# A gated-delta and attention layer on one core: x handed over feature-major, and row sums in four column groups of TensorE

## The reference

```
mod = silu(c) @ ada_w + ada_b                 # c: [1, 1024], ada_w: [1024, 3072]
shift, scale, gate = split(mod, 3)
h = rmsnorm(x, pre_norm_w) * (1 + scale) + shift
proj = h @ w_in                               # 1024 x 4104: q, k, v, gate of 8 attention heads;
                                              # q, k, v, z of 4 delta heads; beta, decay
o_moba = causal attention (rope on q and k) * silu(mg)
o_dn   = rmsnorm(gated delta rule(short_conv(dq, dk, dv))) * silu(dz)
y = concat(o_moba, o_dn) @ w_out
x = x + gate * rmsnorm(y, post_norm_w)
```

## Time and profile before

| | |
|---|---|
| median of 3 runs | 201.45 us (200.59 to 201.94) |
| the profiled execution's own time | 201.38 us |
| its span in the trace | 199.2 us |
| TensorE busy | 185.7 us, 93% |
| VectorE busy | 138.4 us, 69% |
| ScalarE busy | 104.1 us, 52% |
| GpSimd busy | 83.4 us, 42% |
| read from HBM | 37.08 MB |

### The profile page before, as it was taken

The page is one execution under the profiler, slowest core; times in us unless marked ns, Lnnn a source line. Parts: engine busy times, 40 slices in busy tenths (PEclk is TensorE's granted clock), DMA queues, the critical chain, the costliest instruction groups (busy, mean ns, idle before and its releaser), DMA issues.

```text
span 199.2 us, 4716 instructions
## 1 busy us (share of the span) xinstructions
PE 185.7 (93%) x1898; PEld 170.3 (86%) x1898; DVE 138.4 (69%) x326; ACT 104.1 (52%) x201; POOL 83.4 (42%) x46
## 2 busy tenths in 40 slices
PE   7999779999999989999999999997999999899970
PEld 6897769999999989988989999896999987588850
DVE  0638989463079988979878646746989399837364
ACT  2835445636398869396553226385234548337230
POOL 2037709795969616928065003974000220504000
PEclk9988999999999999999999999999999999999998
DMA  5999999999106530197308400062029357910022
GB/s 211 394 403 404 409 396 407 400 406 408 42 0 207 175 147 0 44 396 305 105 3 273 151 3 3 3 212 106 3 74 412 151 205 223 359 59 0 3 107 105
DMA packets 11527, 38.43 MB, mean 193 GB/s; under 512 B 1393, under 2 KB 1521, under 8 KB 10994
## 3 DMA queue, kind: packets, MB, share of 16 engines
q1 hardware_dynamic: 11362, 37.61, 50.6%
q10 hardware_dynamic: 144, 0.52, 0.7%
HBM read 37.08 MB, written 1.05 MB: 191 GB/s over the span
## 4 chain that ended last, share of the span: by engine, by line
PE 51%; DVE 28%; DMA 8%; ACT 6%; issue 3%; POOL 1%; DVEq 0%; SPq 0%; ACTq 0%; POOLq 0%
PE bank L1337 11%; PE bank L1338 10%; PE bank L1339 10%; DVE cv L951 7%; DVE accg L1139 5%; DMA raw<-in_w_out 4%; PE bank L1348 4%; DVE bank L926 3%; DMA outb<-in_post_norm_w 3%; PE bank L1547 3%; PE bank L1558 3%; PE bank L1535 2%; DVE pr L1114 2%; ACT whi L544 1%; DVE ssq L1003 1%
## 5 line engine op out<-in xcount | busy, mean ns | idle before, releaser
L471 POOL TENSOR_TENSOR wlo<-raw,whi 128x1024 fp32r<-128x1024 f32 (+1 forms) x25 | 57.4, 2317 | 66.7 <-ACT whi L544 66.7
L1337 PE MATMUL bank<-hhi,whi 128*128 128x256 f32 x224 | 65.3, 292 | 3.0 <-DVE hlo L895 2.1
L1338 PE MATMUL bank<-hhi,wlo 128*128 128x256 f32 x224 | 63.6, 284 | 0.0
L1339 PE MATMUL bank<-hlo,whi 128*128 128x256 f32 x224 | 63.5, 283 | 0.0
L1337 PEld LDWEIGHTS bank<-hhi,whi 128*128 128x128 f32 x224 | 43.1, 193 | 5.2 <-DVE hlo L895 2.9
L1338 PEld LDWEIGHTS bank<-hhi,wlo 128*128 128x128 f32 x224 | 43.2, 193 | 0.0
L1339 PEld LDWEIGHTS bank<-hlo,whi 128*128 128x128 f32 x224 | 43.1, 193 | 0.0
L544 ACT ACTIVATE whi<-raw 128x1024 fp32r<-128x1024 f32 (+1 forms) x33 | 33.0, 1026 | 10.6 <-PE bank L1339 7.5
L951 DVE SCALAR_TENSOR_TENSOR cv<-bank,convh,cv 128x255 f32<-128x255 f32 (+2 forms) x36 | 17.0, 481 | 8.6 <-ACT cv L608 7.6
L926 DVE SCALAR_TENSOR_TENSOR bank<-ada,sml,bank 128x512 f32<-128x512 f32 (+1 forms) x24 | 16.5, 687 | 0.7
L485 POOL TENSOR_TENSOR rot<-rot,cst 128x512 f32<-128x512 f32 x4 | 4.4, 1091 | 22.3 <-DVE rot L1081 20.4
(11 more groups left out here) (203 smaller groups left out, 359.0 us busy)
## 6 DMA issues: line engine op xcount, KB each, us to landing
raw<-in_w_rest SPq DMA_DIRECT2D x20, 512.0 KB, 5.1
ada<-in_ada SPq DMA_DIRECT2D x12, 512.0 KB, 8.7
ada<-in_gate_w SPq DMA_DIRECT2D x4, 1024.0 KB, 8.3
raw<-in_w_out SPq DMA_DIRECT2D x8, 512.0 KB, 6.2
ada<-in_ada SPq DMA_DIRECT2D x8, 256.0 KB, 6.1
raw<-in_w_qkv SPq DMA_DIRECT2D x5, 384.0 KB, 7.7
qkvs<-in_w_qkv SPq DMA_DIRECT2D x4, 384.0 KB, 9.2
cv<-in_w_qkv SPq DMA_DIRECT2D x4, 384.0 KB, 13.6
```

The costliest lines, as they stand in the source:

```text
L471: pool.tensor_tensor(split_u(wlo, n), raw_u(n), split_u(whi, n).bitcast(F32), ALU.subtract).then_inc(lo_done, 1)
L1337: pe.matmul(out, a[0][ia], b[0][ib], start=start, stop=False, skip_group_check=skip)
L1338: pe.matmul(out, a[1][ia], b[0][ib], start=False, stop=False, skip_group_check=skip)
L1339: return pe.matmul(out, a[0][ia], b[1][ib], start=False, stop=stop, skip_group_check=skip)
```

## The change

x is handed over turned: a new input `x_turned` [128, 8, 256] holds x feature-major, and it is loaded in four quarters (three by the sync engine, one by ScalarE's queue, which also takes the first constants). The transposes, the token-major scaling and the copies out of PSUM go away. The squares are made by ScalarE (quarters 0 and 1) and VectorE (2 and 3) into `xsq`. The sum over the 1024 features is made by TensorE: for slice k a product with a stationary of 32 columns of ones writes 32 equal rows at partitions 32 (k mod 4), so that the 8 slices fall in four column groups, two in each. ScalarE copies these [128, 256] rows out, and a product of each 128-token half with a column of 1/32 gives the sums by token on the partitions. After root and reciprocal, a product of the reciprocals, broadcast along the free axis, with the identity gives a [128, 256] tile that holds the factor of each token in every row; VectorE multiplies x by it in place, piece by piece (`x_scale(p)`).

c times ada of pieces 0 and 1 is made the same way (`mod_rows`): c_k, broadcast to 32 columns, is the stationary, and the piece's 256 columns move through. ScalarE copies the rows into `acc`, and `mod` multiplies by 1/32 in place of ones. VectorE has no sums to do for these two pieces. For piece 0, ScalarE writes `hhi` straight from x while VectorE makes h in PSUM (`h_first`).

The orders of all five engines are written anew, late parts of the kernel too: loads, low parts (five units' low parts leave VectorE's list and two enter, see `DVE_LO`), the gate sums, the bulk halves and the small products.

```diff
-        DVE_LO = (21, 34, 35, 37, 38, 41, 42, 43)
+        DVE_LO = (14, 21, 39, 41, 42)
...
+            def rows_of_four(b, k, stationary, moving):
+                g = slice(32 * (k % 4), 32 * (k % 4) + 32)
+                return pe.matmul(bank[b][g, 0:256], stationary, moving, start=(k < 4), stop=(k >= 4), skip_group_check=True)
+            def x_rows(k):
+                pe.wait_ge(ones_set, 1)
+                if k < 4:
+                    pe.wait_ge(xsq_done, k // 2 + 1)
+                else:
+                    pe.wait_ge(xsq1_done, (k - 4) // 2 + 1)
+                ins = rows_of_four(5, k, ones[:, 0:32], xsq[:, k, :])
+            def x_sums():
+                pe.wait_ge(dve_init, 1)
+                pe.wait_ge(xrows_copied, 1)
+                for t in range(NT):
+                    ins = pe.matmul(bank[5][:, S + t:S + t + 1], acc[:, 1, t * P:(t + 1) * P], epsc[:, 2:3], start=True, stop=True)
+            def x_spread():
+                pe.wait_ge(front_loaded, 16)
+                pe.wait_ge(xrstd_done, 1)
+                for t in range(NT):
+                    ins = pe.matmul(bank[5][:, S + t * P:S + (t + 1) * P], sml[:, 20 + t:21 + t].to_broadcast([P, P]), ident, start=True, stop=True)
+            def mod_rows(p, k):
+                if p == 0:
+                    pe.wait_ge(sc_done, 1)
+                if p == 1:
+                    pe.wait_ge(mod_read, 1)
+                pe.wait_ge(*ada_ready(p, k))
+                ins = rows_of_four(7, k, sml[:, 24 + k:25 + k].to_broadcast([P, 32]), ada_piece(p)[:, k, :])
...
+            def x_square(b):                                     # ScalarE, b = 0, 1
+                act.wait_ge(x_loaded[b], 16)
+                act.activation(xsq[:, 2 * b:2 * b + 2, :], xT[:, 2 * b:2 * b + 2, :], ACT.Square).then_inc(xsq_done, 1)
+            def x_std():
+                act.wait_ge(dve_init, 1)
+                act.activation(sml[:, 22:23], epsc[:, 0:1], ACT.Sqrt)
+                act.wait_ge(xsum_ready, 1)
+                act.activation(sml[:, 18:20], bank[5][:, S:S + 2], ACT.Sqrt, scale=1.0 / D, bias=epsc[:, 0:1]).then_inc(xstd_done, 1)
...
+            def x_scale(p):                                      # VectorE
+                k0, n = PIECES[p]
+                dve.wait_ge(rs_ready, 1)
+                a = xT[:, k0:k0 + n, :]
+                dve.tensor_tensor(a, a, bank[5][:, S:].unsqueeze(1).to_broadcast([P, n, S]), ALU.mult).then_inc(xn_done, 1)
```

TensorE's order in the front, before and after:

```diff
-            busy(1, 3); busy(3, 8); mod_direct(2); mod_direct(3); busy(2, 1); mod_direct(4); mod(0)
-            mod_direct(5); busy(0, 1); mod_direct(6); mod_direct(7); x_turn(0..3)
-            qkv_products(0); mod(1); qkv_products(1); qkv_products(2); mod(2); ...
+            busy(1, 4); x_rows(0..1); busy(3, 1); x_rows(2..7); busy(3, 1); x_sums(); busy(2, 1)
+            mod_rows(0, 0..3); x_spread(); mod_rows(0, 4..7); busy(1, 1); mod(0); busy(1, 2)
+            qkv_products(0); mod_rows(1, all 8); mod(1); qkv_products(1); qkv_products(2); mod(2); ...
```

VectorE's order in the front:

```diff
-            columns_in(); c_silu(); x_square(); mod_sums(0, 0, 2); x_rstd(); x_scale(); modulate(0)
-            mod_sums(1, 0, 4); h_lo(0); xT_move(3); mod_sums(1, 4, 8); modulate(1); mod_sums(2, 0, 4); h_lo(1)
-            mod_sums(2, 4, 8); mod_sums(3, 0, 2); modulate(2); mod_sums(3, 2, 4); h_lo(2)
+            c_silu(); x_square(2); x_square(3); columns_in(); x_rstd(); x_scale(0); x_scale(1); modulate(0)
+            h_first(); h_lo(0); x_scale(2); x_scale(3); mod_sums(2, 0, 4); x_scale(4); modulate(1); h_lo(1)
+            mod_sums(2, 4, 8); mod_sums(3, 0, 2); modulate(2); mod_sums(3, 2, 4); h_lo(2)
```

ScalarE's order in the front:

```diff
-            c_tanh_(); x_square(); x_std(); x_scale(); hi(0); modulated(0); h_hi(0); hi(1); hi(2)
-            xT_copy(0); xT_copy(2); modulated(1); xT_copy(1); hi(3); h_hi(1); hi(4); modulated(2); h_hi(2)
-            hi(5); hi(6); hi(7); hi(8); modulated(3); h_hi(3); hi(9); ba_hi()
+            x_square(0); c_tanh_(); x_square(1); xrows_copy(); x_std(); hi(0); rows_copy(0); h_hi(0); hi(1)
+            rows_copy(1); hi(2); modulated(1); h_hi(1); hi(3); hi(4); modulated(2); h_hi(2)
+            hi(5); hi(6); hi(7); ba_hi(); modulated(3); hi(8); h_hi(3); hi(9)
```

Late, on TensorE and on VectorE (excerpts):

```diff
-            half(12); pv(1); x_products(4, 1); x_products(5, 0); scores(2); w_products(0); half(13); half(14)
-            p_turn(2); t_turn(5, 1); z_products(5, 1); u_products(0); x_products(5, 1); pv(2)
+            x_products(4, 1); x_products(5, 0); t_turn(5, 1); z_products(5, 1); half(12); scores(2)
+            w_products(0); half(14); half(13); half(15); p_turn(2); x_products(5, 1); u_products(0); pv(2)
...
-            merge(5, 0); maxima(2); normalise(2); heads_lo(1); mask_z(5, 1); lo(34); merge(5, 1)
-            gate_sums(0, 0, 4); gate_sums(0, 4, 8); gate(1); gated_heads(2)
+            merge(5, 0); gate_sums(0, 0, 4); heads_lo(0); maxima(2); gate_sums(0, 4, 8); normalise(2)
+            mask_z(5, 1); merge(5, 1); gate(1); gated_heads(2)
```

More of the change, by code:

```diff
@@ L79, with build @@
 GROUPS = [MQ, MK, MG, MV, MQ + 256, MK + 256, MV + 256, MG + 256, DZ, DZ + 256]
-def build(nc, x, ada, gate_w, gate_b, post_w, w_qkv, w_rest, w_gates, w_out, const, out):
+def build(nc, x, x_turned, ada, gate_w, gate_b, post_w, w_qkv, w_rest, w_gates, w_out, const, out):
     with ExitStack() as ctx:
@@ L750, in _ @@
             hi(7)
+            ba_hi()
+            modulated(3)
             hi(8)
-            modulated(3)
             h_hi(3)
             hi(9)
-            ba_hi()
             hi(10)
             hi(11)
+            modulated(4)
             hi(12)
-            modulated(4)
             h_hi(4)
@@ L1248, in _ @@
             conv(5)
+            columns()
             conv_silu(4)
-            columns()
             conv_silu(5)
@@ L1263, in _ @@
             mask_z(0, 0)
-            maxima(1)
-            v_tokens(1)
             mask_z(0, 1)
-            rope(2)
-            normalise(1)
             mask_z(1, 0)
@@ L1271, in _ @@
             merge(1, 0)
+            merge(1, 1)
+            maxima(1)
+            rope(2)
+            normalise(1)
             q_decayed(0)
-            merge(1, 1)
+            q_decayed(1)
             mask_z(2, 0)
@@ L1360, in mod_direct @@
-            def mod_direct(k):
-                pe.wait_ge(sc_done, 1)
-                pe.wait_ge(*ada_ready(0, k))
-                for i in range(2):
-                    ins = pe.matmul(bank[7][:, i:i + 1], ada_piece(0)[:, k, i * P:(i + 1) * P], sml[:, 24 + k:25 + k],
-                                    start=(k == DVE_K[0] and i == 0), stop=False, skip_group_check=True)
-                ins.then_inc(direct_done, 1)
+            def rows_of_four(b, k, stationary, moving):
+                g = slice(32 * (k % 4), 32 * (k % 4) + 32)
+                return pe.matmul(bank[b][g, 0:256], stationary, moving, start=(k < 4), stop=(k >= 4), skip_group_check=True)
@@ L1714, in y_products @@
                     ins.then_inc(unit_done, 1)
-            busy(1, 3)
-            busy(3, 8)
-            mod_direct(2)
-            mod_direct(3)
-            busy(2, 1)
-            mod_direct(4)
-            mod(0)
-            mod_direct(5)
-            busy(0, 1)
-            mod_direct(6)
-            mod_direct(7)
-            x_turn(0)
-            x_turn(1)
-            x_turn(2)
-            x_turn(3)
-            qkv_products(0)
+            busy(1, 4)
+            x_rows(0)
+            x_rows(1)
+            busy(3, 1)
+            x_rows(2)
+            x_rows(3)
+            x_rows(4)
+            x_rows(5)
+            x_rows(6)
+            x_rows(7)
+            busy(3, 1)
+            x_sums()
+            busy(2, 1)
+            mod_rows(0, 0)
+            mod_rows(0, 1)
+            mod_rows(0, 2)
+            mod_rows(0, 3)
+            x_spread()
+            mod_rows(0, 4)
+            mod_rows(0, 5)
+            mod_rows(0, 6)
+            mod_rows(0, 7)
+            busy(1, 1)
+            mod(0)
+            busy(1, 2)
+            qkv_products(0)
+            mod_rows(1, 2)
+            mod_rows(1, 6)
+            mod_rows(1, 1)
+            mod_rows(1, 5)
+            mod_rows(1, 3)
+            mod_rows(1, 0)
+            mod_rows(1, 4)
+            mod_rows(1, 7)
             mod(1)
@@ L1742, in _ @@
             qkv_products(8)
+            mod(4)
             qkv_products(9)
-            mod(4)
             qkv_products(10)
@@ L1786, in _ @@
             x_products(1, 1)
-            z_products(2, 0)
             t_turn(2, 0)
             t_turn(2, 1)
+            half(10)
+            half(11)
+            z_products(2, 0)
             z_products(2, 1)
```

373 lines of the change are left out of this document (181 added, 192 removed).

## The result

The change made the kernel slower: 211.19 us (210.24 to 212.70, 4 runs) against 201.14 us (200.59 to 201.94, 4 runs) in the same comparison, a ratio of 1.050 (1.042 to 1.059; the bracket is a 95% interval). The forecast was 198.1, with a range from 196.4 to 201.7. The profiled execution took 210.31 us, its span is 208.4.

A forecast was written before the change was run, and what follows sets the result against it. The front was taken as bound by VectorE's multiply-adds over the ada pieces up to unit 4, then TensorE until the seventies. 201.38 us less 2.1 (front) less 1.2 (late order) gave 198.1, range 196.4 to 201.7.

The forecast's parts named there:

- The late order: Late part, from the scores of pair 2: new orders gain 1.2 us; bounds 1.7 gained and a loss of 1.5.
- That removes the 1.2 us wait.: Head pair 2: VectorE needs 8.5 us, TensorE has 8.7 us of halves, so its wait for the probabilities goes.
- Removes 0.5 us: Near the end: gate sums, post-norm load and gate rows end earlier, removing TensorE's 0.5 us wait for gate rows.
- Rival 3: Late part: low parts beside normalise and gate sums ahead make pair 2 miss by 2 to 3 us: 201; chance 0.12.
- the late term: Late order's share of the sum: 1.7 us less 0.5 for misses, 1.2 us gained; bounded by a loss of 1.5.
- The front: Start of the kernel up to unit 4: its first product starts at 28.2 instead of 30.31, 2.1 us earlier.
- the line of bytes: Front loads: 1792 KB in 4.7 us, 2.6 us per 1000 KB from 10.22 us on, dates the ada pieces' arrival.
- x: Front: x whole at about 6.6, last square till 7.3, reciprocal at 10.2, over 1 us later than before.
- The pieces: Front: ada piece 0's second half at 10.2, piece 2's first half at 16.6; `modulate(1)` ends at 19.1.
- `ba_hi` ahead of `modulated(3)`: After unit 4: waits for a scattered load issued at 24 to 25, which can cost 0.3 us.
- rival 1: Front: column groups take turns, unit 4's product starts at 32.6, total 202.5 us; chance 0.08.
- rival 2: Front: clock stays at half; if only part is slow, unit 0 starts at 15.5, total 200; chance 0.13.

The follow-up runs named there:

- run 5: Changed kernel with hi(28) and lo(28) moved earlier, hi(29) to hi(31) behind `ti_copy(5, 1)`, and `rope_sin(3)` right behind `rope_sin(2)`: 212.19 us, ratio 1.056.
- run 9: Changed kernel with hi(28) and lo(28) moved earlier and GpSimd starting lo(29) only behind both `q_decayed`: 203.01 us, ratio 1.007 to the kernel before.
- run 8: As run 7, with unit 1 loaded behind the first half of piece 2 and `h_lo(1)` filling VectorE's wait for `hhi`: 202.17 us, ratio 1.006.
- run 7: New front with the late orders of the kernel before, and ScalarE's dummy root with its table load ahead of `xrows_copy`: 201.70 us, ratio 1.003.
- run 4: Changed kernel with hi(28) right behind hi(27) and hi(29) to hi(31) behind `ti_copy(5, 1)` on ScalarE, GpSimd's list untouched: 214.33 us, ratio 1.064.
- run 12: Front of the kernel before with the change's late orders, lo(28) ahead of `rope_sin(2)`, lo(29) to lo(31) behind both `q_decayed`: 201.30 us, ratio 1.002.
- run 11: Kernel before with `p_turn(2)` behind `t_turn(5, 1)` and `z_products(5, 1)`, and `ti_copy(5, 1)` ahead of `pT_copy(2)`: 200.09 us, ratio 0.994.

## Why the prediction was wrong, step by step

**The late order, the step that failed.** The prediction counted instructions and durations only "from the scores of pair 2", and took 1.2 us as gained. It never walked the stretch ahead of it, and so put its cost at nothing. There the change puts hi(28) to hi(30) right behind `probs(1)` and so three low parts beside `normalise(1)`. That stretch cost 6.9 us: `w_products(0)` at 138.16 against 131.24 with the low parts kept clear. The trace has it as 5.4 us of wait and 1.8 of half clock (from the products behind `mask_z(2, .)` to the start of `p_turn(1)` it takes 4.99 us, 120.94 to 125.93; in run 5, at full clock, 3.21), together 0.3 more than the difference. Of the 9.15 us on `w_products(0)`, 0.95 is two pieces that the change moves ahead of it (taken back later); 0.3 was there at `p_turn(0)`; some 1 us is not traced.

**"That removes the 1.2 us wait."** Wrong. The scalings of `normalise(2)` were taken at 3.3 us "even if as slow as" before; in the changed kernel two of them were held instead of one, they took 5.31 us, and the wait became 1.4. At 3.3 us there would have been none, by an estimate from these rows: the scalings end at 149.33, 2.0 us less is 147.3, and TensorE asked at 148.0. In the profiled run 9 they took 3.21 and TensorE did not wait. The change takes five low parts from VectorE and puts them on the engine that holds it.

**"Removes 0.5 us" at the gate rows.** The wait at `accg` went, and one of 1.4 us at `on` came: `outb` landed 1.56 us after VectorE asked for it. From `w_products(0)` to the end both kernels take 64.1 us.

**Rival 3** named the mechanism, low parts beside normalise, and the earlier trace rows had its price in it: four small scalings at 3.31 us. But it looked for the collision at pair 2, where I put it at 2 to 3 us, and bounded the late term at a loss of 1.5, "as bad as the wait it replaces". I didn't work it out as one low part (2.4 us) for each instruction held. By that, three of four scalings held are 7.2 us and more, and 7.27 was measured.

**The front.** Forecast 28.2 for unit 4's first product, measured 30.18; nearly all of the 2.1 us was missing. The term that failed is the line of bytes, which was drawn from 10.22 us of the old trace on and taken to hold for a new start. In the first 10 us the changed kernel reads 157 and then 364 GB/s, the kernel before 211 and 393; why isn't shown. *x* was expected whole at 6.6 with the last square till 7.3. Its last quarter landed at 7.64, the last square ended at 8.36, and the reciprocal came at 11.34 instead of 10.2. *The pieces*: the second half of piece 0 landed at 12.06 instead of 10.2, the first half of piece 2 at 18.34 instead of 16.6, its first two blocks at 17.05. VectorE's scalings, expected done at 15.0, ended at 16.69, and then it waited 0.46 us for these blocks. So `modulate(1)` ended at 21.20 instead of 19.1 and the gain was gone. The wait of about 1 us for `hhi` behind it came as forecast (1.05). A step that the prediction gave 0.3 us, `ba_hi` ahead of `modulated(3)`, cost about that: ScalarE waited 1.94 us for its weights at 34.97, hi(8) came late, and TensorE waited 0.43 us at unit 8.

**What held.** Column groups run side by side (eight records in 0.65 to 0.74 us, sixteen in 1.08), against rival 1. The clock did not stay at half in the front of the changed kernel (two records of ones took 0.70 us at 6.35), against rival 2. In run 8 it did: two records of ones took 1.22 us up to 16 us, and unit 4 came at 32.47. So rival 2 was possible, and its absence here is partly luck. The table load was on x's path at 1.28 us and no more (9.66, the next instruction at 10.96); moving it away gained nothing (run 7).

## What to carry to other kernels

Before work is shifted to GpSimd, or its list is changed, lay its long instructions beside VectorE's list and mark VectorE's additions, scalings and multiply-adds that work in SBUF alone: each of them can cost a whole GpSimd instruction (in run 4 an addition took 2.80 us instead of 0.69 beside a low part of 2.40). TensorE's clock may add to that (here 1.8 us on a wait of 5.4). A stretched small instruction in the trace of before (3.31 us for four scalings that elsewhere take 1.01) is the price list for this. A wait that starts GpSimd in a stretch of PSUM-reading work avoids the collision (runs 9 and 12, where the four scalings of `normalise(1)` took 1.01 us). Where one stays, steps of TensorE that need nothing from VectorE, put ahead of the waiting one, cover most of it (run 11: 0.2 us of wait left of 1.2).

## What the hardware showed that I had not expected

GpSimd's low part, 2.4 us, holds a VectorE instruction until it ends: additions (0.69 to 2.8 us), scalings in two forms (four in 1.01 to 7.6), gate sums (four in 3.12 to 9.01). `mask_z` and `merge`, which read PSUM, keep their 0.29 us beside it. Not all work in SBUF is held: in the kernel before, a sum along the free axis from `th` to `stat`, both in SBUF, runs at its usual 0.69 us inside a low part, and so does the reciprocal of `stat` at 0.17.

```profile
170.31 0.69 DVE L1165 TENSOR_REDUCE stat<-th 128x4 f32<-128x512 f32 x1
```

```profile
169.87 2.57 POOL L471 TENSOR_TENSOR wlo<-raw,whi 128x1024 fp32r<-128x1024 f32 x1 [9.41 <-ACT whi L544]
```

The additions and gate sums read two tensors in SBUF, the scalings of `tensor_scalar` one and a column of factors, the sum along the free axis one. Each held instruction ends just behind a low part: the first scaling of `normalise(1)` in the changed kernel at 114.57 us, the low part beside it at 114.48; the addition of run 4 at 114.37, the low part at 113.82; the first gate sum of run 5 at 131.86, the low part at 131.31. Why the scalings are held and the sum is not, no run here shows.

The column of the granted clock can read 1.00 for want of a record. In run 8 it does so from 6 to 16 us, while two records of ones took 1.22 us instead of 0.70; the trace has its first record of the clock at 16.6 us. In the front the durations tell the clock, not the column.
